# A hybrid encoder block on one core: first loads in joined pieces, regrouped small products and state reads, and the first expert places refilled in transfers of 1 MB

## The chip, the core and the metric

The kernel runs on one core of a Trainium2 chip. The metric is device time in microseconds (us); less is better. The core has a matrix engine (PE), a vector engine (DVE), an activation engine (ACT), a general engine (POOL) and a queue engine (SP) that issues most of the DMA transfers. PE writes only to PSUM, eight banks of 512 float32 for each of 128 partitions; DVE or ACT copy the products out. All data are float32. A float32 matmul stands in the trace as two records on PE.

## The reference, cut to what matters

```
T, D, E, F = 256, 1024, 32, 1024
def reference(x, mem, ...):
    xn = rms_norm(h, norm1_g)
    proj = xn @ w_in                                # 13 column chunks of 256: in0 .. in12
    p = proj[..., :SHIFT_COLS]
    p = p + (token_shift(p) - p) * mu               # r, k, v, wd, ad, gd
    w = -softplus(-(w0 + tanh(wd) @ w2)) - 0.5
    a, g = sigmoid(a0 + ad @ a2), sigmoid(gd) @ g2
    kk = k * k_k / norm_of_each_head(k * k_k)
    k = k * (1.0 + (a - 1.0) * k_a)
    for each step t, each head:                     # recurrent state S, 64 x 64
        sa = S @ -kk_t
        S = S * decay_t + sa (kk_t a_t)^T + v_t k_t^T
        y_t = S @ r_t
    y_rwkv = (group_norm(y) + bonus) * g
    y_diff = diff_attn_group(q, k, v, ...)          # 4 heads, two softmaxes each
    h = h + concat(y_rwkv, y_diff) @ w_out
    h = h + cross_attn(rms_norm(h), rms_norm(mem, mem_norm_g))   # kv = memn @ wkv
    h = h + moe(rms_norm(h), ...)                   # top 4 of 32 experts, clamped SwiGLU
    return rms_norm(h, final_g)
```

## The kernel before

**Stages.** One program computes the block in order. `w_in`, `wkv_x`, `w_out`, `wq_x` and `wo_x` are cut into chunks of 256 columns (1 MB each: 128 partitions, 8 k-slices, 256 columns). `ORDER` lists them: in2, in3, in6, in0, in1, in4, in5, in7 to in12, then kv0 to kv5, out0 to out3 and so on. A chunk is loaded into one of three ring slots (`PRE` = 3), SP waiting for the product of the chunk three places earlier (line 462). `turned(label, src)` multiplies a chunk, 16 matmuls of 256 columns: first all 8 k for the first 128 output columns, then all 8 for the second, into one PSUM bank. Chunks in2, in3 and in6 are multiplied with x times its gain (`gx`) before the norm is known; `factors("x", ..)` then spreads 1/rms over the columns, and DVE scales these products (`scale_products`). `shift` adds the token shift.

**The beginning.** x turned and chunk in2 come in three pieces each ("thirds", lines 474 and 475: k 0-1, 2-3, 4-7), then the rows of x (1 MB), in3, mem (1 MB), in6, mem turned (1 MB) and small tensors. `factors("mem", ..)` stands behind in6, and DVE scales mem turned right after the squares for the head norms (`scale_turned`).

**Head norms and the recurrent part.** `ksum` (line 1033) sums the squares of each head, `kb` (line 1059) spreads the inverse norms back; between them stand in1, the lora products (lines 1046 and 1052: names lw, la, lg) and in4. `L` (line 1079) multiplies inside each chunk of 32 tokens once DVE has raised `ab_ready`; ACT writes L to DRAM in eight small DMAs and reads it back, DVE inverts 16 x 16 blocks (`X16`), and eight more DMAs (line 766) bring the result to `XTb` (semaphore `XT_in`). z1, z2 and z3 (line 1168) need it. The state goes through 8 chunks of 32 tokens: `step(c)` (line 1247) multiplies, DVE adds, and `read_state(c)` (line 1262) reads each state for the output as soon as it is there. Parts of kv2 and kv3 stand between the steps as filler.

**Experts.** Each of 32 experts has three units of 4.19 MB (two of w1, one of w2), each four slots of 1 MB; five places hold a unit each, and a spare one of two slots makes 11 halves. `first_layer` is line 1519, `second_layer` line 1559. PE multiplies all units in order; SP loads unit n when PE has released its place (`released`). Units 6 to 10 are loaded in halves of 2 MB (`half_unit`, line 511), each waiting for a half that PE has left; from unit 11 on whole units (line 445), and from unit 16 on each waits for the whole unit n - 5.

## Time and profile before

| | |
|---|---|
| time, median of 3 runs | 1248.64 us (1248.36 to 1252.04) |
| the profiled execution | 1247.27 us, span 1245.4 us |
| PE busy | 1198.3 us (96%) |
| PE weight loads busy | 573.0 us (46%) |
| DVE busy | 310.5 us (25%) |
| ACT busy | 197.1 us (16%) |
| DMA | 445.52 MB, mean 358 GB/s |

The span runs from the first to the last instruction of the profiled execution. Busy shares are means over stages: the first 338 us compute the mixers and the attention, the rest are the experts.

### The profile page before, as it was taken

Reading aid. Unit: us, or ns where it says so; the run is one execution under the profiler, and the core shown is the slowest. Engines: PE = TensorE matmul, PEld = TensorE weight load, DVE = VectorE, ACT = ScalarE, POOL = GpSimd, SP = SyncE. Lnnn points to the kernel's source line nnn. Section 1 sums busy time; section 2 is a strip of 40 time slices with the busy share of each in tenths; the row PEclk is TensorE's granted clock in tenths of the full one; section 3 lists DMA queues with packets and bytes.
Section 4 is the critical chain, followed back from the end, with each engine's and each line's share of the span. In section 5 each row is a group of like instructions: output and inputs, shape, how many; then the busy total and the mean of one; then the engine's idle time right before and its main releaser. Section 6 shows DMA issues by size and latency. Waiting matters only on the chain.

```text
span 1245.4 us, 17482 instructions
## 1 busy us (share of the span) xinstructions
PE 1198.3 (96%) x7452; PEld 573.0 (46%) x7452; DVE 310.5 (25%) x771; ACT 197.1 (16%) x371; POOL 14.4 (1%) x56
## 2 busy tenths in 40 slices
PE   7998999999999999999999999989999999999998
PEld 6787878888733333333333333323333333333333
DVE  5774245203411211121121112111112211111212
ACT  2313243011211111111111111111111111111101
POOL 4000000000000000000000000000000000000000
PEclk9999999999999999999999999999999999999999
DMA  9332213937799999999999999999999999999995
GB/s 326 133 119 79 103 70 105 415 156 274 300 383 436 418 410 436 429 430 433 429 431 435 428 434 431 430 434 431 430 434 430 433 433 431 430 434 431 426 426 230
DMA packets 29922, 445.52 MB, mean 358 GB/s; under 512 B 8432, under 2 KB 8816, under 8 KB 11440
## 3 DMA queue, kind: packets, MB, share of 16 engines
q1 hardware_dynamic: 24944, 443.74, 84.8%
q10 hardware_dynamic: 4928, 1.05, 0.4%
q8 instruction: 39, 0.64, 0.2%
q14 instruction: 11, 0.09, 0.0%
HBM read 443.47 MB, written 1.31 MB: 357 GB/s over the span
## 4 chain that ended last, share of the span: by engine, by line
PE 71%; DMA 25%; ACT 2%; DVE 1%; issue 1%; ACTq 0%; SPq 0%; DVEq 0%
PE ps L1519 22%; DMA ring<-in_moe_w 15%; PE ps L1559 14%; PE ps L960 10%; DMA arena<-in_moe_w 9%; PE ps L981 7%; PE ps L1463 4%; PE ps L1437 3%; PE ps L1422 2%; PE ps L1451 1%; ACT arena L908 1%; PE ps L1168 1%; PE ps L1456 1%; PE ps L995 1%; DMA ring<-in_w_in 1%
## 5 line engine op out<-in xcount | busy, mean ns | idle before, releaser
L1519 PE MATMUL ps<-ring,arena 128*64 128x512 f32 x1248 | 273.6, 593 | 13.8 <-DMA ring<-in_moe_w 13.2
L1519 PE MATMUL ps<-arena 128*64 128x512 f32 x792 | 174.0, 593 | 8.5 <-DMA arena<-in_moe_w 8.5
L1519 PEld LDWEIGHTS ps<-ring,arena 128*64 128x64 f32 x1248 | 88.9, 137 | 194.2 <-issue 173.2
L1559 PE MATMUL ps<-ring,arena 128*64 128x512 f32 x576 | 127.7, 595 | 0.0
L900 ACT ACTIVATE arena<-arena 128x512 f32<-128x512 f32 x31 | 19.5, 629 | 678.8 <-DVE arena L2119 678.8
L2119 DVE TENSOR_SCALAR arena<-ps 128x512 f32<-128x512 f32 x31 | 21.4, 691 | 397.3 <-PE ps L1519 397.3
L960 PE MATMUL ps<-arena,ring 128*128 128x256 f32 x480 | 107.9, 385 | 8.0 <-DMA ring<-in_w_in 8.0
L1519 PEld LDWEIGHTS ps<-arena 128*64 128x64 f32 x792 | 56.4, 137 | 123.4 <-issue 109.6
L960 PEld LDWEIGHTS ps<-arena,ring 128*128 128x128 f32 x480 | 91.4, 192 | 22.0 <-issue 7.9
L1559 PE MATMUL ps<-arena 128*64 128x512 f32 x408 | 90.7, 595 | 0.4 <-DMA arena<-in_moe_w 0.4
L2132 DVE COPY arena<-ps 128x512 f32<-128x512 f32 x32 | 22.1, 692 | 234.9 <-PE ps L1559 234.9
L1559 PEld LDWEIGHTS ps<-ring,arena 128*64 128x64 f32 x576 | 39.8, 137 | 86.6 <-issue 86.6
L1463 PE MATMUL ps<-arena,rws 64*128 64x512 f32 x256 | 63.6, 615 | 0.2 <-DVE arena L2132 0.2
L1437 PE MATMUL ps<-arena 128*64 128x512 f32 x248 | 60.1, 605 | 0.0
L1559 PEld LDWEIGHTS ps<-arena 128*64 128x64 f32 x408 | 28.2, 137 | 61.6 <-issue 60.3
L2100 DVE TENSOR_TENSOR arena<-ps,prm 128x512 f32<-128x512 f32 x32 | 22.1, 691 | 87.7 <-PE ps L1451 85.5
L981 PE MATMUL ps<-ring,arena 128*128 128x256 f32 x192 | 42.6, 381 | 0.0
L1463 PEld LDWEIGHTS ps<-arena,rws 64*128 64x128 f32 x256 | 22.0, 186 | 40.7 <-issue 40.2
L693 ACT ACTIVATE arena<-ps 128x512 f32<-128x512 f32 (+1 forms) x39 | 21.9, 574 | 118.2 <-PE ps L960 52.3
L900 ACT ACT_TABLE_LOAD x31 | 39.8, 1283 | 1.3 <-issue 0.7
L981 PEld LDWEIGHTS ps<-ring,arena 128*128 128x128 f32 x192 | 36.2, 190 | 5.2 <-issue 0.4
L1422 PE MATMUL ps<-arena 32*64 32x512 f32 x264 | 35.9, 613 | 0.0
(308 smaller groups left out, 866.2 us busy)
## 6 DMA issues: line engine op xcount, KB each, us to landing
ring<-in_moe_w SPq DMA_DIRECT2D x51, 4096.0 KB, 35.2
arena<-in_moe_w SPq DMA_DIRECT2D x32, 4096.0 KB, 36.7
arena<-in_moe_w SPq DMA_DIRECT2D x12, 2048.0 KB, 27.3
ring<-in_moe_w SPq DMA_DIRECT2D x11, 2048.0 KB, 32.8
ring<-in_w_in SPq DMA_DIRECT2D x12, 1024.0 KB, 5.6
ring<-in_wkv_x SPq DMA_DIRECT2D x8, 1024.0 KB, 4.8
ring<-in_w_out SPq DMA_DIRECT2D x4, 1024.0 KB, 4.7
ring<-in_wq_x SPq DMA_DIRECT2D x4, 1024.0 KB, 7.2
```

Source lines behind the costliest of these rows:

```text
L693: drain(s.activation(dst, view(src) if view else src, ACT.Copy), name)
L900: s.activation(dst[:, :], src[:, :], ACT.Sigmoid, scale=1.702).then_inc(sem("sig_ready"), 1)
L960: ins = t.matmul(o[:, q * T:(q + 1) * T], w[:, k, q * P:(q + 1) * P], src[:, k, :], start=(k == 0), stop=(k == KC - 1))
L981: ins = t.matmul(o[:, i * WCOL:(i + 1) * WCOL], src[:, k, i * P:(i + 1) * P], w[:, k, :], start=(k == 0), stop=(k == KC - 1))
L1422: t.matmul(ps[c * BLK:(c + 1) * BLK, 4 + b, :], onehot[g, :], b1a[g, :], start=True, stop=False, tile_position=((2 * b + c) * E, c * BLK), ...
L1437: ins = t.matmul(ps[c * BLK:(c + 1) * BLK, 6, :], sel[:, i, :], h[:, i, c * 512:(c + 1) * 512], start=(i == 0), stop=(i == NT - 1), skip_g ...
L1463: t.matmul(ps[:, 2 * i + c, :], GT[rows, i * P:(i + 1) * P], yy[rows, :], start=False, stop=False, skip_group_check=True)
L1519: ins = t.matmul(ps[c * BLK:(c + 1) * BLK, 4 + b, :], xeT[:, col:col + BLK], w(k % 4)[:, f0:f0 + 512], start=False, stop=(k == KC - 1), sk ...
L1559: ins = t.matmul(ps[c * BLK:(c + 1) * BLK, 7, :], src[:, col:col + BLK], w(k // 2)[:, f0:f0 + 512], start=(k == 0), stop=(k == KC - 1), sk ...
L2100: v.tensor_tensor(xeT[:, :].rearrange("p (m c t) -> p m c t", m=4, c=2), ps[:, 6, :].rearrange("p (m c t) -> p m c t", m=4, c=2), gains, A ...
L2119: v.tensor_scalar(gg[:, :], ps[:, 4, :], 7.0, None, ALU.min).then_inc(sem("gate_ready"), 1)
L2132: v.tensor_copy(yy[:, :], ps[:, 7, :]).then_inc(sem("yy_ready"), 1)
```

## The change

It has four parts.

- **Beginning.** The host packs x turned and chunk in2 into one tensor, slice by slice, and five pieces bring k 0, 1, 2-3, 4-5 and 6-7 of both. in2 no longer uses a ring slot. Its matmuls run with k outside: for each k both output halves, into two banks. in3 follows the pieces, then the rows of x, in6 and in0; mem and mem turned come behind in1. `factors("x")` stands behind the whole of in3, `factors("mem")` behind in9; ACT squares mem behind in7's copy, DVE scales mem turned behind the first score maxima, with factors that ACT has copied to SBUF.
- **Order in the recurrent part.** ksum's four matmuls go to four groups of 32 output partitions, kb's four to four groups of 32 input rows and four banks, directly behind the lora products. in7 is multiplied behind L. DVE does `shift(4)`, the remainders (`t34`) and the k update behind `ab_ready`. ACT copies the natural rows before it issues the XTb DMAs, and the MV products before the first exps.
- **State reads.** `read_states(i)` reads four states at once, behind step 3's filler and behind the last step, where eight single reads stood; `centre(0)` is in step 6.
- **Refill.** Units 6 to 10 are loaded slot by slot, 1 MB each, and each waits for its own slot (`slot_emptied`, with new increments of `slot_used` in both layers).

```diff
+FIRST_PIECES = (slice(0, 1), slice(1, 2), slice(2, 4), slice(4, 6), slice(6, 8))
...
                 if n == 0:
-                    for m, (k0, k1) in enumerate(thirds):
...
+                    for m, ks in enumerate(FIRST_PIECES):
+                        sp.dma_start(first[:, ks, :], a["first"][:, ks, :]).then_inc(sem(f"first{m}_in"), 16)
                     continue
...
-            def half_unit(n, half):
+            def half_unit(n, half, emptied=lambda p, m: None):
                 p = 2 * n + half - 11
-                dst = units[p // 2][:, p % 2 * H:(p % 2 + 1) * H]
-                sp.dma_start(dst, unit(n, half)[1]).then_inc(place_landed[p], 16)
+                for m in range(2):
+                    emptied(p, m)
+                    at = (2 * (p % 2) + m) * SLOT
+                    src = unit(n, half)[1][:, m * SLOT:(m + 1) * SLOT]
+                    sp.dma_start(units[p // 2][:, at:at + SLOT], src).then_inc(place_landed[p], 16)
+
+            def slot_emptied(p, m):
+
+                e, t, k = p // 2 // PER, p // 2 % PER, 2 * (p % 2) + m
+                if t < 2 and k % 2 == 0:
+                    sp.wait_ge(sem("slot_used") if t else sem("between_used"), 4 * e + (1 + k // 2 if t else 2 + k // 2))
+                elif t == 2 and k % 2 == 0:
+                    sp.wait_ge(sem("slot_used"), 4 * e + 3 + k // 2)
+                else:
+                    released(p // 2, k // 2)
...
+            w = weights("in2")
+            o = [begin(pe, f"in2{q}") for q in range(2)]
+            for k in range(KC):
+                for m, ks in enumerate(FIRST_PIECES):
+                    if k == ks.start:
+                        pe.wait_ge(sem(f"first{m}_in"), 16)
                 pe.wait_ge(sem("gx_ready"), k + 1)
+                for q in range(2):
+                    ins = t.matmul(o[q][:, 0:T], w[:, k, q * P:(q + 1) * P], gx[:, k, :], start=(k == 0), stop=(k == KC - 1))
...
             for j in range(NP):
-                ins = t.matmul(o[0:NH, 0:T], hsel[:, j, :], t2[:, j, :], start=(j == 0), stop=(j == NP - 1))
+                ins = t.matmul(o[j * CH:(j + 1) * CH, 0:T], hsel[:, :, :].rearrange("p a b -> p (a b)"), t2[:, j, :], start=True, stop=True,
+                               tile_position=(0, j * CH))
...
+            pe.wait_ge(sem("knorm_ready"), 1)
+            o = [begin(pe, f"kb{j}") for j in range(NP)]
+            for j in range(NP):
+                rows = slice(j * CH, (j + 1) * CH)
+                done(t.matmul(o[j][:, 0:T], hselT[rows, :], krs[rows, :], start=True, stop=True, tile_position=(j * CH, 0)), f"kb{j}")
             turned("in4", xT)
...
+                for j in range(NP):
+                    for c in range(P // CH):
+                        for q in range(2):
+                            rows = slice(q * HD, (q + 1) * HD)
+                            tok = slice(i * P + c * CH, i * P + (c + 1) * CH)
+                            ins = t.matmul(o[q][c * CH:(c + 1) * CH, j * HD:(j + 1) * HD], RhT[rows, j, tok], St[rows, 4 * i + c, j, :],
+                                           start=True, stop=True, tile_position=(q * HD, c * CH))
```

On PE, at the beginning of the program (`L960` is `turned`, `L1008` the factors, `L1033` ksum, `L1046` and `L1052` the lora products, `L1059` kb, `L1079` L), before:

```order
L960 MATMUL ps<-arena,ring 128x256 x24
L1008 MATMUL ps<-arena,ones 128x128 x2
L960 MATMUL ps<-arena,ring 128x256 x24
L1008 MATMUL ps<-arena,ones 128x128 x2
L960 MATMUL ps<-arena,ring 128x256 x16
L1033 MATMUL ps<-arena,extra 8x256 x4
L960 MATMUL ps<-arena,ring 128x256 x16
...
L1052 MATMUL ps<-arena 128x256 x2
L960 MATMUL ps<-arena,ring 128x256 x16
L1059 MATMUL ps<-arena,extra 128x256 x4
L960 MATMUL ps<-arena,ring 128x256 x32
L1079 MATMUL ps<-arena 32x32 x64
```

And in the changed kernel (`L1060` is in2, `L999` `turned`, `L1047` the factors, `L1072` ksum, `L1092` the last lora products, `L1098` kb, `L1117` L):

```order
L1060 MATMUL ps<-arena 128x256 x16
L999 MATMUL ps<-arena,ring 128x256 x16
L1047 MATMUL ps<-arena,ones 128x128 x2
L999 MATMUL ps<-arena,ring 128x256 x32
L1072 MATMUL ps<-arena,extra 32x256 x4
L999 MATMUL ps<-arena,ring 128x256 x16
...
L1092 MATMUL ps<-arena 128x256 x2
L1098 MATMUL ps<-arena,extra 128x256 x4
L999 MATMUL ps<-arena,ring 128x256 x32
L1117 MATMUL ps<-arena 32x32 x64
```

The factors of x moved from the middle of in3 to its end, those of mem out of this stretch, kb from behind in4 to ahead of it, and L ahead of in7.

On ACT, from the copies of L (`ring<-ps 128x8x32`) to the first z copies; `L745` and `L766` are the small DMAs of L and XTb, `L679` are the squares, `L779` the exps and `L693` copies, before:

```order
L693 ACTIVATE ring<-ps 128x8x32 x2
L745 DMA blocks<-ring 16x16x16 x8
L693 ACTIVATE arena<-ps 128x512
L755 DMA arena<-blocks 128x256
...
L761 DMA blocks<-arena 128x256
L693 ACTIVATE arena<-ps 128x512
L766 DMA ring<-blocks 16x16x16 x8
L693 ACTIVATE arena<-ps 128x8x64
L693 ACTIVATE arena<-ps 128x512
L798 ACTIVATE lam<-lam 128x2
L779 ACTIVATE ring,extra<-ps,extra 128x128 x8
L693 ACTIVATE arena<-ps 128x8x64 x2
```

And in the changed kernel (`L723` copies, `L774` and `L804` the small DMAs, `L781` the squares of mem, `L816` the exps):

```order
L723 ACTIVATE ring<-ps 128x8x32 x2
L774 DMA blocks<-ring 16x16x16 x8
L723 ACTIVATE arena<-ps 128x512
L781 ACTIVATE ring,st<-ring 128x1024 x2
L723 ACTIVATE arena<-ps 128x512
L790 DMA arena<-blocks 128x256
...
L723 ACTIVATE arena<-ps 128x8x64
L723 ACTIVATE arena<-ps 128x512
L804 DMA ring<-blocks 16x16x16 x8
L835 ACTIVATE lam<-lam 128x2
L723 ACTIVATE arena<-ps 128x8x64 x2
L816 ACTIVATE ring,extra<-ps,extra 128x128 x8
```

The XTb DMAs moved behind the second natural rows, the exps behind the MV copies, and the squares of mem came in from the beginning.

On PE, at the state steps (`L1247` a step, `L960` a filler of four matmuls, `L1262` a read, `L995` the transposes of the last attention weights, `L1139` their values), before:

```order
L1247 MATMUL ps<-arena,ring 64x64 x8
L960 MATMUL ps<-ring 128x256 x4
L1262 MATMUL ps<-arena 32x64 x16
L1247 MATMUL ps<-arena,ring 64x64 x8
L960 MATMUL ps<-ring 128x256 x4
L1262 MATMUL ps<-arena 32x64 x8
L1247 MATMUL ps<-arena,ring 64x64 x8
L995 MATMUL ps<-ident,ring 128x128 x4
L960 MATMUL ps<-ring 128x256 x4
L1262 MATMUL ps<-arena 32x64 x8
L1247 MATMUL ps<-arena,ring 64x64 x8
L1139 MATMUL ps<-arena 128x128 x4
```

And in the changed kernel (`L1287` a step, `L999` a filler, `L1299` the reads):

```order
L1287 MATMUL ps<-arena,ring 64x64 x8
L999 MATMUL ps<-ring 128x256 x4
L1287 MATMUL ps<-arena,ring 64x64 x8
L999 MATMUL ps<-ring 128x256 x4
L1287 MATMUL ps<-arena,ring 64x64 x8
L1034 MATMUL ps<-ident,ring 128x128 x4
L999 MATMUL ps<-ring 128x256 x4
L1299 MATMUL ps<-arena 32x64 x32
L1287 MATMUL ps<-arena,ring 64x64 x8
L1179 MATMUL ps<-arena 128x128 x4
```

The reads of the first two states, of the third and of the fourth moved together, behind the transposes and their filler.

## Rows read from the trace of the kernel before

**Rows 1.** Stretches: engines busy, PE clock, DMA share, GB/s last.
```profile
0.00:10.00 10.00, 2.88 (x7) 2.31 (x8) 1.66 (x5) 1.49 (x2) 7.54 (x30) 1.00 0.73 214
10.00:20.00 10.00, 9.12 (x41) 7.47 (x40) 5.25 (x22) 1.86 (x3) 6.08 (x24) 1.00 1.03 423
361.00:364.00 3.00, 3.00 (x16) 1.01 (x14) 0.00 (x0) 0.00 (x0) 0.00 (x0) 1.00 0.60 169
...
417.00:419.00 2.00, 2.00 (x12) 0.72 (x10) 0.00 (x0) 0.00 (x0) 0.00 (x0) 1.00 0.92 262
...
447.00:449.00 2.00, 2.00 (x12) 0.66 (x10) 1.42 (x5) 0.00 (x0) 0.00 (x0) 1.00 1.00 311
...
500.00:1200.00 700.00, 675.58 (x3216) 226.95 (x3213) 126.72 (x274) 84.94 (x124) 0.00 (x0) 1.00 1.00 431
```

**Rows 2.** Chain that ended last: start us, us, what; expert stage.
```profile
338.22 13.95 PE ps L1519 x64
...
440.52 7.02 PE ps L1559 x32
...
774.86 36.14 DMA ring<-in_moe_w
```

**Rows 3.** SP queue in order of time, 300 to 480 us.
```profile
447.58 14.06 SPq L445 DMA_DIRECT2D ring<-in_moe_w  x3
```

**Rows 4.** Waits of PE over the span: total us, times, longest.
```profile
PE ps L960 <- DMA ring<-in_w_in: 8.0, 2, 7.1
PE ps L1168 <- ACT arena L693: 1.8, 1, 1.8
PE ps L1125 <- ACT arena L693: 1.3, 1, 1.3
```

**Rows 5.** Instructions in order of time, 0 to 45 us: start, us.
```profile
6.48 0.81 DVE L1691 TENSOR_SCALAR arena<-arena,prm 128x256 f32<-128x256 f32 x2 [6.48 <-DMA arena<-in_x_turned]
...
7.12 3.75 PE L960 MATMUL ps<-arena,ring 128*128 128x256 f32 x8 [7.12 <-DMA ring<-in_w_in]
...
11.74 8.87 PE L960 MATMUL ps<-arena,ring 128*128 128x256 f32 x40 [0.88 <-DMA ring<-in_w_in]
...
14.20 1.23 DVE L1693 SCALAR_TENSOR_TENSOR arena<-arena 128x1024 f32<-128x1024 f32 x1 [3.16 <-DMA arena<-in_x]
```

**Rows 6.** The chain again, 38 to 95 us, then rows in order of time.
```profile
38.77 1.82 PE ps L1033 x8
...
47.70 1.06 PE ps L1046 x8
...
58.86 1.92 PE ps L1059 x8
...
93.38 1.41 PE ps L1099 x91
...
51.03 1.85 ACT L720 ACTIVATE arena<-ps,w0h 128x256 f32<-128x256 f32 x4
...
60.03 0.69 DVE L1786 TENSOR_TENSOR arena<-ps,arena 128x512 f32<-128x512 f32 x1 [2.23 <-PE ps L1059]
...
72.48 1.23 DVE L1810 TENSOR_TENSOR arena<-arena 128x1024 f32<-128x1024 f32 x1
```

**Rows 7.** ACT issuing DMAs; issues by line with us to landing.
```profile
101.94 4.16 ACTq L766 DMA_DIRECT2D ring<-blocks  x8
...
blocks<-ring ACTq DMA_DIRECT2D x8, 16.0 KB, 2.4
...
ring<-blocks ACTq DMA_DIRECT2D x8, 16.0 KB, 4.4
```

**Rows 8.** The chain, 155 to 200 us: state steps and reads.
```profile
171.41 0.83 PE ps L1262 x32
...
176.10 0.66 PE ps L995 x4
...
178.49 0.57 PE ps L1262 x16
```

More of the change, by code:

```diff
@@ L148, in program @@
         Bd, Kd = cut(BK0, NP, T), cut(BK0 + 1024, NP, T)
-        xdiag, mdiag = (cut(BK0 + NT * P * n, NT, P) for n in range(2))
+        xdiag, mdiag = cut(BK0, NT, P), side(6, NT, P)
+        fm = side(6, T)
+        first = cut(AR0, KC, T + WCOL)
         gT = cut(GT0, NP, T)
@@ L277, in program @@
         place("x_factors", 2)
-        chunk("in2")
+        for q in range(2):
+            place(f"in2{q}", 6 + q)
+        where["in2"] = where["in20"]
         chunk("in3")
-        place("mem_factors", 3)
         chunk("in6", 4)
@@ L288, in program @@
             place(f"lg{n}", 6 + n)
+        for j in range(NP):
+            place(f"kb{j}", 2 + j)
         chunk("in4")
-        for n in range(2):
-            place(f"kb{n}", 2 + n)
         for n in (5, 7, 8, 9, 10):
@@ L406, in home, with ring_uses @@
         def home(n):
+            if ORDER[n] == "in2":
+                return first[:, :, T:T + WCOL]
             return cut(apart[ORDER[n]], SLOT) if ORDER[n] in apart else ring[:, n % PRE, :]
         landed = [sem(f"slot{s}_landed") for s in range(PRE)]
+        def ring_uses(n):
+            return sum(1 for m in range(n % PRE, n + 1, PRE) if m)
         place_landed = [sem(f"place{p}_landed") for p in range(2 * SLOTS)]
@@ L747, in _ @@
                    .then_inc(sem("L_blocks_out"), 16)
+            copy(qd[:, 0:2, :], "in7", two)
+            act.wait_ge(sem("mem_in"), 16)
+            for i in range(NT):
+                link(s.activation(mem_squares[:, :], memN[:, i, :], ACT.Square, accum_out=st[:, i:i + 1]))
+            act.sem_inc(sem("stat_ready"), 1)
             def natural_rows(i):
@@ L1082, in _ @@
                                 done(ins, f"L{q}")
+            turned("in7", xT)
             turned("in8", xT)
@@ L1108, in _ @@
             turned("in9", xT)
+            factors("mem", mdiag)
             chunk_products(1)
@@ L1731, in shift @@
                         link(ins)
-                dlink(ins, f"in{m}")
+                if m == 2:
+                    link(ins)
+                    for q in range(2):
+                        dve.sem_inc(drained[where[f"in2{q}"][0]], 1)
+                else:
+                    dlink(ins, f"in{m}")
                 dve.sem_inc(sem("shifted_ready"), 1)
@@ L1811, in _ @@
             dve.sem_inc(sem("ab_ready"), 1)
+            shift(4)
+            product(dve, "lg1")
+            for j in range(NP):
+                ins = v.tensor_tensor(t34[:, j], tail[:, j, :].unsqueeze(2).to_broadcast([P, NCH, CH]), cs4[:, j], ALU.subtract)
+            link(ins)
+            dve.sem_inc(sem("rest_ready"), 1)
             shift(5)
+            link(v.scalar_tensor_tensor(out=kT[:, :, :], in0=KT[:, :, :], scalar=1.0, in1=kT[:, :, :], op0=ALU.add, op1=ALU.mult))
             link(v.tensor_tensor(KT[:, :, :], kT[:, :, :], t1[:, :, :], ALU.mult))
@@ L1889, in _ @@
             score_max(0)
+            dve.wait_ge(sem("memT_in"), 16)
+            dve.wait_ge(sem("mem_factors_in"), 1)
+            taken(dve, "mem_factors")
+            for k in range(KC):
+                r = ROW["mem_norm_g"] + k
+                ins = v.scalar_tensor_tensor(out=memT[:, k, :], in0=memT[:, k, :], scalar=prm[:, r:r + 1], in1=fm[:, :],
+                                             op0=ALU.mult, op1=ALU.mult)
+            ins.then_inc(sem("memT_ready"), 1)
             dve.wait_ge(sem("lam_exp_ready"), 1)
```

199 lines of the change are left out of this document (85 added, 114 removed).

## The prediction

> **What bounds the kernel now.** I read the stretches first [rows 1]. From 500 to 1200 us the DMA share is 1.00 at 431 GB/s, so the expert stage is the reading of 96 weight units of 4.19 MB. The chain of waits [rows 2] says the same from the other side: from 338.22 us it is matmuls of the experts alone, one expert each 27.3 us, and the first DMA piece in it (36 us of waiting for a unit) stands at 774.86; from there on every second expert has one. So PE is the slower of the two first only because DMA has units in hand.
>
> The end is then the moment from which the stream never stops, plus bytes over rate. I looked for the last stop. The stretches [rows 1] have DMA dips at 361 to 364 us (169 GB/s), 417 to 419 (262) and 447 to 449 (311), and none behind. The SP queue [rows 3] tells what ended the last one: SP issues three whole units from 447.58 us, and PE's second layer of expert 3 ends at 440.52 + 7.02 = 447.54 [rows 2]. The place that is filled is the one that PE has just left; the next four units lie in SBUF. Behind it come 80 units: 335.5 MB at 431 GB/s are 778 us, 449 + 778 = 1227 us, where the stream ends. Until 447.5 us **PE's own order binds**, and what counts is how much earlier PE comes to expert 0 (338.22 us [rows 2]). A DMA gap before 447 is worth nothing, as long as it doesn't reach past that release.
>
> Before 338 us PE is the bound almost everywhere: its waits [rows 4] are 8.0 us for the first weights, 1.8 and 1.3 us for ACT, and shorter ones behind these in the same list. So a gain is matmul time taken out, or one of these waits.
>
> **The start.** PE begins at 7.12 us with 8 records of 3.75 us, stands 0.88 us for the last third, and from 11.74 us 40 records take 8.87 us [rows 5]: 0.47 us a record against 0.22 (a matmul of 256 float32 columns is two records). The clock column has 1.00 for 0 to 10 us [rows 1]; the records' spacing is that of 1.2 GHz, half the later one. Before: 4 of the 16 matmuls of in2 are done at 10.9, 12 are left at 11.74, 12 x 0.43 = 5.2, end 16.9 us. After: both halves take piece k as it comes, and no matmul waits for the last piece. Piece 0 has the size of the first x third, which the first DVE scaling used at 6.48 us [rows 5]; with 0.4 us of scaling PE begins at 6.9. At 0.85 us a matmul 4.7 are done by 10.9, 11.3 x 0.43 = 4.9 follow, end 15.8 us. **Gain 1.1 us**. With all matmuls at the later rate it would be bound by the pieces: 14.2 us and a gain of 2.7 us, which is the upper bound; the lower is 0 (the first piece lands as late as the first weights did and the slow stretch is longer).
> The Trainium skill (TensorE: Matmul & The Clock Gate, What's actually happening) says that the default state is throttled and activity releases it, so that matmuls put earlier run at half rate; by that rule, the trace's 0.47 against 0.22 us agrees, and its 1.00 in the clock column doesn't.
> The rows of x come after in3 now. Before, their second half was in DVE's hands at 14.20 us [rows 5] and the factors' diagonal ready 4.5 us later. One 1 MB load (2.4 us at 423 GB/s) ahead of them makes that 21.1 at most; PE wants it at 22.7, behind in3. The moved mem factors (0.44 us of PE, 3.2 us of DVE) leave the path before in0 and come back behind in9: nothing in all. With both mem steps gone DVE is through shift 3 at 30.0 us and PE at in0 at 30.2, so no new wait.
>
> **ksum, kb and their bank.** ksum is 8 records in 1.82 us, one after the other [rows 6]. Now the four matmuls stand in four column groups of 32. That such groups run together shows in the chunk products, where 128 records of 64 columns on 64x32 pieces take 1.41 us [rows 6] (alone, at a quarter of the 0.22 us for 256 columns, they would take 7), and in the expert layer, where 64 records of 512 columns in pairs of column groups take 13.95 us [rows 2], 0.22 each, half of what 512 columns cost alone. I take 0.6 us, gain 1.2. kb is 8 records in 1.92 us [rows 6], now four row groups into four banks: 0.6, gain 1.3. Both bounds: 0 (no overlap) and 1.4. The cost: kb follows the lora products at once and needs banks 2 to 5, the last of them emptied by ACT's second la tanh. ACT's pair began at 51.03 and took 1.85, to 52.88 us, 5.2 us behind the first lora product (47.70) [rows 6]; PE is done after 4.25 us. New wait: 0.95 us; queued behind it are in4 and in5. Together **+1.55 us**.
>
> **The DVE chain to ab_ready.** L is now in front of in7, 7 us sooner. Before, its last step ended at 72.48 + 1.23 = 73.7 us [rows 6]. Shift 4 (1.1), the t3 step (1.4) and the four kT sums (1.7) are taken out ahead of it, the wait for kb (2.23 us, to 60.03 [rows 6]) goes, and so does that of exp for unshifted 4. Summed from the same durations (of a step of 1024 columns 1.23 us, of four steps of 256 columns 1.4 to 1.8): lora at 44.8, lw ready 49.2, aa 55.0, kk 56.6, AR 58.2, KT 59.8, aa 61.0, AR 62.9, BT 64.2 us. PE is there at 64.5. It fits with 0.3 us to spare; what DVE loses more is paid by PE one to one. ops_ready moves to 73 us and isn't wanted before 81.
>
> **The middle (in10 to z1).** Before: in10 ends 101.9, scores wait 1.34 us for ACT, which was issuing 8 DMAs (101.94 to 106.1), and z1 waits 1.85 us for ACT's MV copies behind 3.9 us of exps [rows 4, 7]. Both orders are turned round, both waits end (3.2 us). What is late next is XT_in: the DMAs now follow the natural rows, so issue runs from 101.1 to 105.3 us, and 2.4 (the L blocks, alone) to 4.4 us (the median here, beside a weight load) more until they land [rows 7]. PE's wait for them stands before in11, at 106.3. I take 107.7: 1.4 us of new wait. So z1 begins at 111.4 instead of 115.96. Lead 4.5 us: 2.65 from above, 3.2 - 1.4 = 1.8 here. Bounds: 3.9 to 5.1; beyond that exps(0), now behind the copies, hold the banks of z1 until 110.3.
>
> **State reads.** Eight reads are 3.9 us of PE (0.83 for two, 0.57 for one [rows 8]), each with only two row groups at work. In two groups of 32 matmuls on eight pieces each takes 0.8 us, half of the chunk products' 1.41 plus the change of form: 1.6 us instead of 3.9. But attn_ready(2) is the next bound: PE now has the transposes at 176.10 just as DVE ends the combine [rows 8]. Without two reads, step 2 is 0.8 us earlier, so is the combine, and PE waits 0.65. Sum **+1.6 us** (0.8 to 2.3). The last filler covers the state steps on DVE (1.3 us each under 1.9).
>
> **The refill.** The 9 halves of 2 MB become 18 transfers of 1 MB, each released when its slot is used. The stop within 361 to 364 us [rows 1] ends one slot earlier (four of the second layer's 16 matmuls, 7.02 / 4 = 1.75 us). By the above this is **0** at the end: at 417 and 447 DMA stands waiting for the same release of PE, only longer. Two increments more per layer ride on matmuls that run anyway. That such transfers keep the rate: from 10 to 20 us only loads of 0.5 to 1 MB were under way, and 423 GB/s moved at a share of 1.03 [rows 1].
>
> Sum: 1.1 + 1.55 + 1.8 + 1.6 = 6.05, say 6.1 us. Span 1245.4 - 6.1 = 1239.3. The profiled run was 1247.27 us in all, 1.9 over its span; the median of the runs shown is 1248.64, 3.2 over it. Forecast 1239.3 + 3.2 = **1242.5 us**.
>
> **Rivals.**
> 1. The refill counts after all: if the stops at 417 and 447 were not PE's releases but transfers under way, the 1.7 us are kept: 1242.5 - 1.7 = 1240.8. For: the dips are short, 2 x (1 - 262/431) = 0.8 and 2 x (1 - 311/431) = 0.6 us [rows 1]. Against: 447.54 and 447.58. Chance 0.10.
> 2. The start is worth 2.7 us and XT_in lands in time: 1242.5 - 1.6 - 1.4 = 1239.5. Chance 0.10.
> 3. Cover too thin: DVE comes 1 us late to ab_ready, packing gives half (1.2 less), XT_in lands at 108.4 (0.7 more) and the state reads bring 0.8 less: lead 2.4, 1246.2. All four places have thin cover and the sum of shares doesn't show them. Chance 0.18.
> 4. Slower: the 1 MB transfers don't hold the rate. Place: 341 to 417 us, 21.0 MB in 20 of them. At 431 GB/s they are 48.7 us; spare are the 1.7 us and the dips of 0.8 and 0.6, 3.1 in all. The end is later than before if they lose over 6.1 + 3.1 = 9.2 us, a rate of 21.0 / 57.9 = 363 GB/s or less. The lowest rate in a row is 0 to 10 us: 214 GB/s at a share of 0.73, 293 at a full one [rows 1]. By it they take 71.7 us, 23.0 more, and the time is 1248.6 + 23.0 - 9.2 = 1262.4. Against: those are pieces of 2 KB rows, and the queue now always holds several transfers, since PE frees a slot in 1.75 us and DMA fills one in 2.4. Chance 0.04.
> The Trainium skill (DMA: Bandwidth & Descriptors, Measured) gives 341 GB/s for a transfer of 1 MB against 425 for 16 MB; by that rate the time would be an estimated 1252. The 423 GB/s of 10 to 20 us speak against it for queued transfers.
> The forecast has the rest, 0.58, with 1240 to 1245 as its own range.
>
> **How the numbers follow.** A measurement here tells about 0.3% (3.7 us) from no change: 1244.9. Faster: rivals 1 and 2 and nearly all of the forecast's case, 0.20 + 0.54 = 0.74, with 0.02 of rival 3: 0.76. Same: 0.16 of rival 3 and 0.04 of the forecast's: 0.20. Slower: rival 4, 0.04. The range takes rivals 1 to 3 in: from 1237.8 (the first two together) to 1246.8.
>
> **What would show it.** In the profile after: expert 0's first layer near 332 us instead of 338.22, the DMA dip at 447 near 441 and as long or longer; in2's matmuls without a wait after the first, still 0.47 us a record before 11 us; 8 ksum records within 0.7 us; a wait near 49 us on ACT's tanh and one of 1 to 2 us on the XT transfers near 106; the gap at 362 shorter by 1.7 us with the same end. I am wrong if expert 0 is early and the end isn't, or if the end moves more than expert 0 does; and the sum is mis-sized where a step's lead, read at the beginnings of in0, the lora products, z1 and kv4 and at the end of in5, leaves it: 1.6, 2.9, 4.5, 6.1 and 3.2 us.

## The result, and the profile after

The changed kernel takes 1240.52 us (median of 5 runs, 1239.01 to 1242.07) beside 1248.64 for the kernel before on the same chip: a ratio of 0.9931, 95% interval 0.9911 to 0.9951. It is faster by 0.7%, 8.1 us. Its profiled run took 1240.43 us with a span of 1238.7; the span is 6.7 us shorter.

I go along PE first. The chain of waits of the changed kernel, with start and length in us:

```profile
1.27 3.21 DMA arena<-in_first
...
4.58 0.49 DVE arena L1721
...
5.20 9.92 PE ps L1060 x32
15.12 6.91 PE ps L999 x32
...
29.64 7.14 PE ps L999 x32
36.78 0.57 PE ps L1072 x8
37.35 7.10 PE ps L999 x32
44.46 1.07 PE ps L1086 x7
...
49.78 0.71 PE ps L1098 x8
...
103.75 3.44 DMA ring<-blocks
107.23 3.72 PE ps L1020 x16
110.95 3.63 PE ps L1208 x128
...
169.94 0.66 PE ps L1034 x4
...
172.32 0.79 PE ps L1299 x53
...
186.05 6.91 PE ps L1020 x32
...
331.10 13.95 PE ps L1553 x64
...
1174.67 38.02 DMA arena<-in_moe_w
```

L1060 is in2, L1072 ksum, L1086 the lora products, L1098 kb, L1208 z1, L1299 a group of state reads, the L1020 at 186.05 kv4, L1553 the first layer of expert 0. Three beginnings of the kernel before that stand in no group (in0, z1, kv4):

```profile
31.87 6.91 PE ps L960 x32
...
115.96 3.69 PE ps L1168 x128
...
193.17 6.91 PE ps L981 x32
```

With these and [rows 2, 6] the leads are: in0 31.87 - 29.64 = 2.2 us, lora 47.70 - 44.46 = 3.2, z1 115.96 - 110.95 = 5.0, kv4 193.17 - 186.05 = 7.1, expert 0 338.22 - 331.10 = 7.1. The row at 1174.67 is the last landing that PE waits for, that of the second half of the last unit but one (the two halves of the last unit land behind it, at 1217.6 and 1222.5 us, ahead of PE's use). It comes at 1174.67 + 38.02 = 1212.7 instead of 1219.4: there 0.4 us of the lead is gone. Where I or the expectations below say "the last landing", this one is meant.

PE's longest waits (us in total, times, longest):

```profile
PE ps L1553 <- DMA ring<-in_moe_w: 13.3, 8, 1.7
...
PE ps L1060 <- DVE arena L1721: 5.2, 1, 5.2
PE ps L1020 <- DMA ring<-blocks: 1.1, 1, 1.1
PE ps L1098 <- ACT arena L750: 1.1, 1, 1.1
...
PE ps L1034 <- DVEq L1919: 0.7, 1, 0.7
```

The two ACT waits of [rows 4] are gone, and each of the three that was forecast stands there: for the tanh (L750), for the XT transfers (ring<-blocks), and for the combine (L1919).

SP's queue, in order of time, and six stretches (the columns as in [rows 1]: last the clock, the share of DMA and GB/s):

```profile
336.51 22.46 SPq L534 DMA_DIRECT2D ring<-in_moe_w  x10
360.36 12.35 SPq L534 DMA_DIRECT2D arena<-in_moe_w  x8
...
440.48 0.33 SPq L466 DMA_DIRECT2D ring<-in_moe_w  x1
```

```profile
10.00:20.00 10.00, 10.00 (x46) 8.74 (x45) 4.71 (x20) 1.15 (x2) 5.80 (x27) 1.00 1.01 402
...
354.00:355.00 1.00, 1.00 (x7) 0.29 (x5) 0.00 (x0) 0.00 (x0) 0.00 (x0) 1.00 0.81 164
355.00:356.00 1.00, 1.00 (x8) 0.43 (x6) 0.00 (x0) 0.00 (x0) 0.00 (x0) 1.00 0.72 262
...
440.00:441.00 1.00, 1.00 (x8) 0.29 (x4) 0.51 (x1) 0.00 (x0) 0.00 (x0) 1.00 0.38 164
...
444.00:500.00 56.00, 55.78 (x270) 18.91 (x268) 10.20 (x22) 6.95 (x10) 0.00 (x0) 1.00 1.00 431
500.00:1200.00 700.00, 675.76 (x3222) 227.26 (x3220) 126.66 (x274) 85.51 (x124) 0.00 (x0) 1.00 1.00 431
```

The release that was at 447.58 [rows 3] is at 440.48, 7.1 us earlier as expert 0 is, and the dip of DMA stands behind it at 440. The one at 361 to 364 is now at 354 to 356, and shorter by the shares (not by bytes, as the first experiment shows). From 444 us on the stream runs at 431 GB/s as before.

### The profile page after: what moved, and what is told of

The parts are those of the page before. It is cut to its first block, busy times and chain, and to the rows that moved or that the text cites. A ratio compares the mean times of both kernels' runs of the same rounds, so it can differ in the third digit from the quotient of the medians.

```text
span 1238.7 us, 17505 instructions
## 1 busy us (share of the span) xinstructions
PE 1194.5 (96%) x7452; PEld 570.7 (46%) x7452; DVE 309.9 (25%) x768; ACT 197.8 (16%) x372; POOL 14.7 (1%) x59
## 3 DMA queue, kind: packets, MB, share of 16 engines
q10 hardware_dynamic: 4928, 1.05, 0.4%
## 4 chain that ended last, share of the span: by engine, by line
PE 71%; DMA 25%; ACT 2%; DVE 1%; issue 1%; ACTq 0%; DVEq 0%; SPq 0%
PE ps L1553 22%; DMA ring<-in_moe_w 15%; PE ps L1595 14%; PE ps L999 10%; DMA arena<-in_moe_w 9%; PE ps L1020 7%; PE ps L1497 4%; PE ps L1471 4%; PE ps L1456 2%; PE ps L1485 1%; ACT arena L945 1%; PE ps L1208 1%; PE ps L1060 1%; PE ps L1490 1%; PE ps L1034 1%
## 5 line engine op out<-in xcount | busy, mean ns | idle before, releaser
L1553 PE MATMUL ps<-ring,arena 128*64 128x512 f32 x1248 | 273.6, 593 | 13.9 <-DMA ring<-in_moe_w 13.3
L1553 PE MATMUL ps<-arena 128*64 128x512 f32 x792 | 174.0, 593 | 8.3 <-DMA arena<-in_moe_w 8.2
L1553 PEld LDWEIGHTS ps<-ring,arena 128*64 128x64 f32 x1248 | 88.9, 137 | 194.3 <-issue 173.2
L1553 PEld LDWEIGHTS ps<-arena 128*64 128x64 f32 x792 | 56.4, 137 | 123.2 <-issue 109.6
L999 PE MATMUL ps<-arena,ring 128*128 128x256 f32 x448 | 98.8, 380 | 0.3 <-DVE arena L1756 0.3
L999 PEld LDWEIGHTS ps<-arena,ring 128*128 128x128 f32 x448 | 84.5, 190 | 12.8 <-issue 1.4
L1020 PE MATMUL ps<-ring,arena 128*128 128x256 f32 x192 | 42.6, 381 | 1.1 <-DMA ring<-blocks 1.1
L723 ACT ACTIVATE arena<-ps 128x512 f32<-128x512 f32 (+1 forms) x39 | 21.9, 575 | 112.6 <-PE ps L999 51.0
L1020 PEld LDWEIGHTS ps<-ring,arena 128*128 128x128 f32 x192 | 36.2, 190 | 6.4 <-DMA ring<-blocks 1.3
```

Of the source, the lines that this page charges most:

```text
L723: drain(s.activation(dst, view(src) if view else src, ACT.Copy), name)
L999: ins = t.matmul(o[:, q * T:(q + 1) * T], w[:, k, q * P:(q + 1) * P], src[:, k, :], start=(k == 0), stop=(k == KC - 1))
L1020: ins = t.matmul(o[:, i * WCOL:(i + 1) * WCOL], src[:, k, i * P:(i + 1) * P], w[:, k, :], start=(k == 0), stop=(k == KC - 1))
L1553: ins = t.matmul(ps[c * BLK:(c + 1) * BLK, 4 + b, :], xeT[:, col:col + BLK], w(k % 4)[:, f0:f0 + 512], start=False, stop=(k == KC - 1), sk ...
```

## The experiments

Times are medians on the chip. The kernel before, which ran beside each of three sets, had 1248.95, 1249.88 and 1248.61 us; a ratio is always that to the kernel before of the same set. For the single stages I read the profiled run of each kernel.

### The refill: undone, and alone

```diff
 # a_old_refill: the changed kernel
-                for m in range(2):
-                    emptied(p, m)
-                    ... 1 MB each
+                released(*divmod(2 * n + half - 11, 2))
+                sp.dma_start(dst, unit(n, half)[1]).then_inc(place_landed[p], 16)
 # b_refill: the kernel before, with the - lines
```

> The changed kernel with the refill undone alone: the nine halves are again transfers of 2 MB, each waiting for both of its slots. My theory: nothing at the end. PE comes to expert 0 at 331.1 us as in the changed kernel, PE's second layer of expert 3 ends at 440.44 and the whole units are issued at 440.48; the stop of DMA near 354 us is about 1.1 us longer (2.1 instead of 1.0), the one behind 440 stays 0.8 to 1.0 us, the span is 1238.7 (within 0.4) and the ratio to the kernel before 0.993. Rival (the refill counts): the 1.7 us of the stop are lost at the end too, span 1240.4, ratio 0.9945.

Measured: 1240.24 us (1238.99 to 1242.21, 6 runs), ratio 0.9923 (0.9903 to 0.9943), against 0.9931 with the new refill. The stop of DMA, in the same stretches as above:

```profile
354.00:355.00 1.00, 1.00 (x6) 0.29 (x4) 0.00 (x0) 0.00 (x0) 0.00 (x0) 1.00 1.06 442
355.00:356.00 1.00, 1.00 (x8) 0.41 (x6) 0.00 (x0) 0.00 (x0) 0.00 (x0) 1.00 0.50 197
356.00:357.00 1.00, 1.00 (x8) 0.30 (x6) 0.00 (x0) 0.00 (x0) 0.00 (x0) 1.00 0.12 49
```

By the shares it is 1.4 us of standing instead of 0.5 (1 minus the shares, summed), and the time is no longer. The profiled span was 1240.4, as the rival had it, but not by its cause: expert 0 began at 331.98 (not 331.1) after a stretch of low clock (last section), which is 0.9 us of it, and the other 0.8 are those of one slow DMA engine (the table of engines below).

By bytes the new refill doesn't even shorten the stop. The stretch around it, and the one behind it in which the pieces stream, with the new refill and then with the old:

```profile
350.00:362.00 12.00, 12.00 (x62) 4.17 (x64) 2.40 (x6) 1.71 (x2) 0.00 (x0) 1.00 0.95 349
362.00:386.00 24.00, 23.89 (x118) 8.09 (x115) 3.47 (x7) 3.47 (x5) 0.00 (x0) 1.00 1.01 424
...
350.00:362.00 12.00, 11.89 (x64) 4.37 (x64) 2.41 (x6) 2.46 (x3) 0.00 (x0) 1.00 0.89 356
362.00:386.00 24.00, 23.89 (x118) 8.11 (x116) 3.40 (x6) 3.48 (x5) 0.00 (x0) 1.00 1.02 434
```

349 and 356 GB/s beside 431 are 2.3 and 2.1 us of transfers lost, nearly the same. So these two runs alone can't tell whether DMA time is free here or whether the new refill saves none; the extra transfer of the next section can.

> The kernel before with the new refill alone (18 transfers of 1 MB, each released when its slot is used; two increments more in a layer). My theory: expert 0 at 338.2 us, the release that SP waits for at 447.5, span 1245.4 within 0.4, ratio 1.000; the stop at 361 to 364 us ends about 1.7 us sooner. Rival 1 (the refill counts): span 1243.7, ratio 0.9986. Rival 4 (transfers of 1 MB lose rate): span over 1245.9 and the stop behind 447 gone.

Measured: 1248.76 us (12 runs) against 1248.95, ratio 0.9996 (0.9983 to 1.0009), span 1246.3. The new refill alone is worth nothing that can be measured, in either direction. Rival 4 of the prediction falls: the transfers of 1 MB moved at 424 GB/s where those of 2 MB had 434 (rows above), far from 363, and nothing of it reaches the end. Rival 1 is not excluded by the time alone (1.7 us less would be 0.9986, just inside the interval), but undone the refill costs nothing either, and from PE's release to L the median engine takes the same with it and without it (table below).

### Where a microsecond of DMA counts

```diff
 # dummy_early: behind the two halves of unit 6;  dummy_late: behind unit 20
+    sp.dma_start(scratch[:, :], a["moe_w1"][E - 1, 1][:, 0:SLOT]).then_inc(sem("scratch_in"), 16)
```

> The changed kernel with one transfer of 1 MB more (from the weights to a scratch area in DRAM), issued behind the refill of unit 6, near 341 us. My theory (only what PE releases at 440.5 us counts): DMA's stops near 354, 410 and 440 us are 2.15 us together and take it up; the release stays at 440.48, the span moves by 0 to 0.4 us (1238.7 to 1239.1). Rival (every microsecond of DMA counts): the span is 2.4 us longer, 1241.1, whatever is idle behind it.

> The changed kernel with the same extra transfer of 1 MB, now issued behind unit 20, near 540 us, where DMA never stands. My theory: here every microsecond of DMA counts. From the start of expert 0 to the last landing of a weight (881.6 us in the changed kernel, 881.2 with the extra transfer near 341 us) it takes 2.4 us more, 883.6 to 884.0. Rival (a transfer of 1 MB into DRAM is cheap wherever it stands, and the early one told nothing): 881 to 882 us here too.

Measured: early 1241.11 us (ratio 0.9931), span 1239.1, from expert 0 (331.92) to the last landing (1213.12) 881.2 us, where the changed kernel has 881.6: 1 MB more for nothing. Late (it was issued at 474.47 us, not near 540): 1243.45 us (0.9949), and 330.57 to 1214.41 is 883.84 us, 2.3 to 2.6 more. In the early run the stop at 354 is filled:

```profile
354.00:355.00 1.00, 1.00 (x8) 0.34 (x6) 0.00 (x0) 0.00 (x0) 0.00 (x0) 1.00 1.00 401
355.00:356.00 1.00, 1.00 (x8) 0.38 (x6) 0.00 (x0) 0.00 (x0) 0.00 (x0) 1.00 1.04 410
```

So the prediction's reading holds: before PE's release at 440 DMA time is free up to the length of its stops, behind it each microsecond is paid in full (1 MB at 431 GB/s is 2.4 us).

### The refill's idea carried on

```diff
-            for n in range(FIRST, FIRST + SLOTS):
-                released(n - SLOTS, 0)
-                load(n)
+            for n in range(FIRST, UNITS_ALL - PAIR):
+                load_parts(n, emptied=released)   # n < 20: two halves, each behind the last reader of its place
```

> The changed kernel with the refill's idea carried on to the units behind it: units 11 to 19 are loaded in halves (the first half of unit 15 in quarters), each issued as soon as the place under it is used up, so that the first half of unit 16 goes when PE is half through the second layer of expert 3 (3.5 us before 440.48). My theory (the end is set by the stops at 410 and 440 us): both stops, 0.35 and 0.8 us, are gone, and the stretch from expert 0 to the last landing is 1.15 us shorter than in the changed kernel: 881.6 to 880.4 (single profiles of this stretch scatter by about 0.5). Rival (the rate of the stream is the limit and the stops are made good by fuller engines behind them): 881.2 to 881.8.

Measured: 1239.71 us (6 runs), ratio 0.9925 (0.9907 to 0.9943); 330.61 to 1212.63 is 882.0 us. The theory failed. The stops at 410 and 440 us are both gone; the issue that waited for 440.48 now stands at 436.55, and the stretch behind the old dip is full:

```profile
436.55 7.20 SPq L480 DMA_DIRECT2D ring<-in_moe_w  x3
...
440.00:442.00 2.00, 2.00 (x12) 0.65 (x10) 1.69 (x5) 0.00 (x0) 0.00 (x0) 1.00 1.02 434
```

and the end didn't move. By bytes the stream was 2 us earlier; the last landing was not. That led to the question what "the end of the stream" is.

### Sixteen engines, and the slowest of them

Each of the 16 DMA engines writes a mark of its own when its share of a transfer is done, and the record keeps these marks. Per transfer I took the time of the last mark behind the median of the 16: for the late 4 MB units, and for the transfer whose landing is L. G is the end of the second layer of expert 3 (PE's release), L the last landing that PE waits for; all in us, one profiled run each:

```
kernel         G        L        L - G    last engine behind median   L - G - lag
                                          late units      at L        at L
before         447.54   1219.41  771.9    1.9             0.7         771.2
after          440.44   1212.69  772.3    1.6             0.9         771.3
a_old_refill   441.32   1214.35  773.0    1.6             1.7         771.3
b_refill       447.86   1220.33  772.5    1.8             1.0         771.4
b_states       447.72   1219.52  771.8    1.6             0.5         771.3
dummy_early    441.24   1213.12  771.9    1.7             0.6         771.3
dummy_late     439.91   1214.41  774.5    2.1             0.8         773.7
kb_inside      442.04   1214.07  772.0    1.9             0.8         771.3
xt_behind      439.22   1213.64  774.4    4.3             3.1         771.3
a_q_outer      442.59   1214.95  772.4    1.9             1.1         771.3
a_two_first    442.19   1216.13  773.9    3.8             2.6         771.3
best2          438.47   1211.13  772.7    2.4             1.2         771.4
fine           439.95   1212.63  772.7    4.2             3.8         768.9
one_engine     444.55   1222.98  778.4    6.8             6.6         771.9
```

Where the gate is PE's release and nothing was added behind it, the last column is 771.2 to 771.4 in all eleven profiles, a_old_refill's too: its 0.8 us more between G and L are the engine that was 1.7 us behind instead of 0.9. The 1 MB more of dummy_late is 2.4 us. What scatters in L - G from 771.8 to 774.4 is how far the slowest engine is behind. In fine the middle engine is 2.4 us ahead (768.9) and the slowest 3.8 us behind it. The marks of single units show where the lag comes from (the four last engines of each unit, us behind the median; first column the median mark), here xt_behind:

```
567.81  1.32  1.50  1.71  2.74
577.52  1.32  1.51  1.70  4.45
587.23  1.33  1.50  1.72  4.31
```

The lag is constant over hundreds of microseconds and jumps by 1 to 1.6 us for one engine at a time. Each jump stands beside one of the 16 KB packets of the instruction queue (39 packets of 0.64 MB in the span of the changed kernel), here that at 579.8 us, which took 1.1 us; the one at 450.6 had put the last engine to 2.75, and those at 476.1 and 501.7 moved others. Between 581 and 1176 us there is no such packet, and the lag doesn't move. In the changed kernel's own profile six such packets between 451 and 581 us fell on several engines, and the last one never was more than 1.7 us behind. Two more, at 1176 and 1201 us, shift the engines once again, so the lag at L is not that of the late units. A stop of the stream lets the engines draw level: in a_old_refill the last one was 2.2 us behind ahead of the stop at 356 us and 0.1 behind it; in fine, which has no stop at 410 and 440, it was 3.5 us behind at 390 us and still 3.4 at 450.

```profile
q8 instruction: 39, 0.64, 0.2%
```

The test gives one engine more work, and the stream next to none:

```diff
 # one_engine: the changed kernel, behind unit 20
+    for m in range(16):
+        sp.dma_start(spare[1][m:m + 1, :], a["moe_w1"][E - 1, 1][m:m + 1, 0:SLOT]).then_inc(sem("rows_again_in"), 16)
```

> The changed kernel with 16 transfers more behind unit 20, each a single row of 8 KB (131 KB in all, 0.3 us of the stream's 431 GB/s). The marks of the DMA engines (each adds its own to the semaphore of a transfer) show that in every run one engine of the 16 ends a unit 1.6 to 4.4 us behind the median, while the mean rate is 97.14 us for ten units in every run. My theory: the end is that of the slowest engine, not bytes over rate. If the rows all go to one engine, it gets 16 x 0.31 = 4.9 us more and the stretch from expert 0 to the last landing (881.6 us) grows by 3.3 to 4.9 us; the mean stream ends within 0.5 us of where it did. Rival (bytes over rate, or rows dealt out among the engines): 0.3 to 0.6 us.

Measured: 1246.41 us (10 runs), ratio 0.9982 (0.9970 to 0.9995): 131 KB cost 5.9 us against 1240.52, where 1 MB spread over all engines cost 2.9. In the profile L - G is 1222.98 - 444.55 = 778.4, 6.2 more than in the changed kernel, and above the 3.3 to 4.9 expected. Counted from G, the median engine's mark at L came only 0.6 us later; the last engine's comes 6.6 us behind it instead of 0.9. The end is that of the slowest engine: shown. (Its profiled run was the slowest of the ten, 1250.75 us: expert 0 began at 334.14 and its first layer took 15.03 us instead of 13.95, by a stretch of low clock. All of that is ahead of G.)
The Trainium skill (DMA: Bandwidth & Descriptors, Why a DMA increments its semaphore by 16 and not by 1) says that a transfer runs on the largest number of engines, up to 16, that divides the slowest dimension on both of its sides, and that transfers of a queue like SP's take the lowest-numbered engines. By that rule a single row that isn't cut up goes to one engine, the same each time. The trace agrees: each of the 16 rows is one packet of 8 KB, and one engine alone is 5.2 us further behind in the late units (6.8 instead of 1.6). What such a transfer costs, here 5.9 us, is its engine's time and not its bytes' share.

### The state reads alone

```diff
 # b_states: the kernel before
-            def read_state(c): ...
+            def read_states(i): ...   # with the calls and the centring at c == 6 as in the change
```

> The kernel before with the new state reads alone (two groups of 32 matmuls on eight pieces instead of eight reads, and the centring one step later). My theory: kv4 and expert 0 begin 2.1 us sooner than in the kernel before (193.17 to 191.1, 338.22 to 336.1; the changed kernel's lead grows by 2.1 to 2.3 us over this stage, where I had forecast 1.6), the release at 447.5 and the end move with it: span 1243.3, ratio 0.9983. Rival: the steps' chain through DVE sets the stage's length, and the reads were in its shadow: kv4 moves by under 0.8 us and the span by as little.

Measured: 1247.24 us (10 runs), ratio 0.9991 (0.9971 to 1.0010). The forecast of the span (1243.3) failed, it was 1245.6, but the stage did what was expected: from z1 to kv4 it is 193.33 - 118.15 = 75.2 us instead of 193.17 - 115.96 = 77.2. The 2.0 us were lost at the start, before the changed lines:

```profile
11.74 10.98 PE ps L960 x40
```

where the same 40 records took 8.87 in [rows 5]. At 0.22 us a record 8.87 is all of them at 2.4 GHz; 2.1 us more are 8 to 9 records at 0.47. The clock came up some 4 us later in this execution of the same instructions; by the trace's record of the granted clock the full level begins at 16.02 us, and at 10.96 in the profile of the kernel before.

### The start: order and size of the first pieces

```diff
 # a_q_outer
-            for k in range(KC):
-                for q in range(2):
+            for q in range(2):
+                for k in range(KC):
 # a_two_first
-FIRST_PIECES = (slice(0, 1), slice(1, 2), slice(2, 4), slice(4, 6), slice(6, 8))
+FIRST_PIECES = (slice(0, 2), slice(2, 4), slice(4, 6), slice(6, 8))
```

> The changed kernel with in2's matmuls again half by half (all eight pieces of the first 128 columns, then of the second), not piece by piece. The gain of the start was forecast at 1.1 us and was 1.8. My theory: it comes from the first piece, in DVE's hands at 4.58 us, and from the slow clock's stretch (0.47 us a record until about 10 us) being worked through sooner, and not from the order: in2 ends at 14.5 to 15.3 us here too (15.12 in the changed kernel's profile), since the last piece is scaled at 10.8 us and PE has half of the matmuls left then. Rival (the order carries it, no matmul waiting for the last piece): 16 us or later, with a wait of 0.5 us or more inside the first half.

Measured: 1242.01 us (2 runs), ratio 0.9953. PE in order of time:

```profile
5.22 2.05 PE L1061 MATMUL ps<-arena 128*128 128x256 f32 x4 [5.22 <-DVE arena L1722]
8.41 9.14 PE L1061 MATMUL ps<-arena 128*128 128x256 f32 x28 [1.15 <-DVE arena L1722]
```

My theory failed, the rival is right: in2 ends at 17.6 us, with a wait of 1.15 us for the third piece. All 28 records at 0.22 would take 6.2 us; the 2.9 more are some 12 at the slow clock, which then lasts to about 14 us (the full level is recorded from 14.20 us), instead of 10.8 in the changed kernel. That the clock came up late because PE stood is possible, but the kernel before had such a late rise too (b_states), so with one profile it stays open. The order is worth the wait of 1.15 us at least.

> The changed kernel with the first two pieces of 256 KB joined to one of 512 KB (four pieces of two instead of five). My theory: small first pieces matter by when PE starts, and little more: the first scaling is at 5.3 to 5.8 us instead of 4.58, and in2 ends 0.3 to 0.8 us later than 15.1, since each 0.47 us record that starts later is one at the slow clock. Rival (the clock's rise goes with PE's start, so everything is moved by the full shift): 0.9 us later or more. Second rival (rows of 2 KB are so slow that joining wins): sooner.

Measured: 1243.01 us (3 runs), ratio 0.9958. 

```profile
6.41 0.86 DVE L1721 TENSOR_SCALAR arena<-arena,prm 128x256 f32<-128x256 f32 x2 [6.41 <-DMA arena<-in_first]
...
7.05 8.79 PE L1060 MATMUL ps<-arena 128*128 128x256 f32 x32 [7.05 <-DVE arena L1721]
```

The first piece is ready at 6.41, 1.8 us later and more than I thought; in2 ends at 15.8, 0.7 later, as the theory had it. That number alone proves little: nine profiles in which this start is unchanged (the changed kernel and eight variants) have in2's end at 13.7 to 15.1 us, because the full clock level is recorded there from 8.3 to 10.8 us. The pair with the same clock tells more. In kb_inside the full level begins at 10.38 us, as it does here; PE starts at 5.56 us there and at 7.05 here, 1.5 us later, and in2 ends at 15.08 and 15.84, 0.8 us later. So half of the delay is paid, and in this pair the clock's rise did not wait for PE's start.

### PE's two remaining waits

```diff
 # xt_behind
-            pe.wait_ge(sem("XT_in"), 16 * (P // SUB))
             value_chunk = natural_parts("in11", xT)
             next(value_chunk)
+            pe.wait_ge(sem("XT_in"), 16 * (P // SUB))
 # kb_inside: kb behind a quarter of in4, L behind a quarter of in7
+            key_chunk = turned_parts("in4", xT)
+            next(key_chunk)
             pe.wait_ge(sem("knorm_ready"), 1)
...
+            cross_chunk = turned_parts("in7", xT)
+            next(cross_chunk)
             pe.wait_ge(sem("ab_ready"), 1)
```

> The changed kernel with the four kb matmuls set inside in4, behind its first quarter, and the L products inside in7, behind its first quarter. My theory: the wait for ACT's tanh (1.05 us) ends, nothing takes its place since ab_ready (64.0 us when the lora products begin at 44.46) is covered by in7's first quarter; from the beginning of the lora products to that of z1 it is 65.5 us instead of 66.5. Rival (DVE's chain to ab_ready binds, cover 0.3 to 0.5 us): a wait of 0.5 us or more before L, and under half of it is gained.

Measured: 1241.57 us (4 runs), ratio 0.9932; from lora (44.42) to z1 (112.00) it is 67.6 us, 1.1 longer. Theory and rival both failed, by a wait that neither had:

```profile
PE ps L999 <- DVE arena L1762: 2.0, 1, 2.0
```

in7 fills the PSUM bank of in4, which shift 4 (L1762) empties, and shift 4 stands behind ab_ready on DVE. The wait of 1.05 us was taken away and one of 2.0 put in its place.

> The changed kernel with PE's wait for the XT transfers set behind the first half of in11. My theory: of the 1.1 us that PE stands at 106.1 us, 0.7 to 1.1 go, since the transfers land at 107.2 and half of in11 runs to 109.6 us; from in0 to z1 it is 80.2 to 80.6 us instead of 81.3. Rival (the exponentials hold the banks of z1 until 110 us, so one wait takes the place of the other): over 81.0 us, with a new wait of z1 for ACT.

Measured: 1240.47 us (6 runs), ratio 0.9932. The first quarter of z1 begins at 109.24 us, 80.1 us behind in0 instead of 81.3, as the theory had it. The other three quarters begin at 110.52: there the rival is right, and PE waits 0.2 us for ACT's exponentials, which hold the banks.

```profile
109.91 0.47 ACT ring L816 x2
110.52 2.82 PE ps L1207 x96
113.34 3.65 PE ps L1020 x16
```

From in0 to the end of z1 it is 84.2 us instead of 84.9; to expert 0 300.7 instead of 301.5. So 0.75 us stay, the low end of my range.

> The changed kernel with the XT wait behind the first half of in11 (0.75 us from in0 to expert 0 in its own run) and the kb matmuls inside in4, behind its first quarter, L staying ahead of in7. My theory: L waits 0.5 us for ab_ready (64.0 us when lora begins at 44.46), where the wait of 1.05 us for ACT was, so 0.5 more is gained: from the beginning of in0 to that of expert 0 it is 300.2 us instead of 301.46. At the end 1.2 us of it show only if the slowest DMA engine follows: ratio to the kernel before 0.992 to 0.993. Rival for the first part (DVE's chain to ab_ready moves with kb): nothing of the 0.5 us.

Measured: 1238.85 us (1238.03 to 1240.65, 5 runs), ratio 0.9929 (0.9916 to 0.9943), span 1237.1. From in0 (29.03) to expert 0 (329.14) it is 300.1 us, as forecast; L waits 0.7 us for DVE where kb waited 1.05:

```profile
PE ps L1120 <- DVEq L1837: 0.7, 1, 0.7
```

It has the lowest median of all, 1.7 us below the changed kernel, which is less than the two medians can tell apart: each ran beside the kernel before in its own set, and the ratios, 0.9929 and 0.9931, are the same. The trace's 1.3 us from in0 to expert 0 are the better measure.

## Why the prediction was right

It had 1242.5 us (1237.8 to 1246.8); 1240.52 was measured. The mechanism held: the lead at expert 0 came through to PE's release at 440 and from there to the end, and the refill was worth nothing. The 2.0 us of difference are these: the leads of PE came to 7.1 instead of 6.1 (1.0 more), 0.4 of it was lost in the last stretch (0.2 by the slowest engine, 0.9 us behind at L instead of 0.7), and 1.4 lie in the reference: the prediction added 3.2 us from span to median, and the changed kernel had 1.8 (the profiled run of before was 1.4 us under its median, that of the changed kernel 0.1). So 1.4 of the 2.0 us are scatter of the runs and no part of the mechanism.

- **The start**: forecast 1.1, measured 1.8 at the end of in2 (15.12 instead of 16.9, which the prediction worked out and no row has; 24 of the 40 records of 8.87 us give 17.1) and 2.2 at in0, of which the forecast had 1.6. The slow stretch to about 10 us was right. Mis-sized was the first piece: PE began at 5.2 and not at 6.9, since that piece, of which I only took the size, landed 3.2 us after its issue. I had set it to the first x third's 6.48 [rows 5]; joining two pieces (a_two_first) gives just that, 6.41. (At in0 the 0.44 us of the mem factors are in both numbers.) The clock is no part of this difference: the full level is recorded from 10.96 us before and from 10.82 after. It also settles the 1.00 of the clock column for 0 to 10 us, which the prediction set against the spacing of the records: the record has no entry ahead of the rise, and the column shows 1.00 where it has none.
- **ksum and kb**: 8 records of ksum in 0.57 us (0.6 forecast), of kb in 0.71 (0.6), the new wait 1.1 (0.95). Not foreseen was a wait of 0.3 us in in0. From in0 to the end of in5 the lead grew by 1.1 (67.8 - 64.5 = 3.3, less 2.2) where 1.6 was forecast.
- **DVE's chain to ab_ready**: 64.0 us forecast 64.2, PE there at 64.5; no wait. best2 shows how thin the cover is: PE 1.05 us sooner waits 0.7 for it.
- **The middle**: from the end of in10 (lead 2.9, forecast 2.65) to z1 (5.0) it is 2.1 us against 1.8. The XT transfers landed at 107.2 instead of 107.7.
- **The state reads**: 2.1 us (7.1 - 5.0) against 1.6, inside the bounds, and 2.0 alone (b_states). A group takes 0.79 us (0.8 forecast), the wait for the combine is 0.7 (0.65). The rest is 0.3 us ahead of the combine, where PE's two stalls before the first steps went from 0.54 and 1.01 us to 0.82 and 0.56 (0.2 of it), and 0.1 behind it: the bounds from single rows didn't have the stalls.
- **The refill**: 0 forecast, 0 measured both ways round. That the stop would be 1.7 us shorter failed: it is 0.9 us shorter by the shares and no shorter by bytes. The step "a DMA gap before 447 is worth nothing" is shown by the early 1 MB. Rival 1 (1240.8 us) is numerically the nearest to the result, but its cause isn't there.
- **"The release, then bytes over rate"** was right in size and incomplete in kind: it is the release, bytes over rate and the slowest engine, 0.5 to 3.8 us behind at the last landing in the kernels without extra rows. That it came out this well is luck in part: the prediction had no such term, and before and after had nearly the same lag (0.7 and 0.9).

What stays open: what decides on which engine an instruction packet falls, and whether a stand of PE after its start delays the clock's rise.

## What to carry to other kernels

When a queue of transfers never stops, find the last stop and what ended it, and don't count DMA time before it; test it with a dummy transfer on either side. Taking the stops away gives nothing if an engine that is behind needs them to catch up: look at the marks of the single engines, and keep single-row transfers out of a full stream. A wait that is removed by putting work ahead of it needs the place that this work writes to be free: look for its last reader in the other engine's order before looking at the gain.

## What the runs showed of the hardware

- One of the 16 DMA engines is 1.6 to 4.3 us behind the median through most of the stream (0.5 to 3.8 at the last landing that PE waits for), by jumps of 1 to 1.6 us beside the 16 KB packets of the instruction queue; 16 rows of 8 KB on one engine cost 5.9 us, 1 MB on all of them 2.9 by the medians and 2.4 by the landings.
- The first pieces: one of 256 KB lands 3.2 us after its issue, one of 512 KB is ready 1.8 us later, though 256 KB at 431 GB/s are 0.6 us.
- The granted clock differs between executions of the same instructions. At the start the slow level (0.47 us a record) ended between 8.3 and 14.2 us in the profiles of the changed kernel and its variants, at 10.96 us in that of the kernel before, and at 16.02 in that of b_states. Near 325 us, in the router, where PE's waits are 0.3 to 0.6 us, it fell in some profiles and not in others, for 1 us of the time. a_old_refill, then the changed kernel:

```profile
324.00:326.00 2.00, 2.00 (x12) 0.99 (x14) 1.09 (x8) 1.67 (x5) 0.00 (x0) 0.50 1.05 451
...
324.00:326.00 2.00, 1.67 (x17) 0.71 (x15) 1.28 (x9) 1.67 (x5) 0.00 (x0) 1.00 0.95 410
```

  0.50 is 1.2 GHz. From kv4 to expert 0 it is 145.05 us without the fall and 146.0 to 146.1 with it (149.6 in one_engine, where it lasted beyond 330 us). With the rise at the start (1.4 us between profiles of the same start) and the slowest engine (up to 3 us), a single profile places an end to a few microseconds only, and a stage away from these places to 0.1.
